# A decoder trunk's first 30 microseconds in another order: memory rows before the small tables, each half of them handled by itself

## The reference

```python
h = x + 0.5 * rms_norm(swiglu(rms_norm(x, n_ffn1_pre), ffn1_w_in, ffn1_w_out), n_ffn1_post)
m = token_mixing(rms_norm(h, n_mix_pre), ...)     # w_in, three branches, w_out
h = h + rms_norm(m, n_mix_post)
h = h + 0.5 * rms_norm(swiglu(rms_norm(h, n_ffn2_pre), ffn2_w_in, ffn2_w_out), n_ffn2_post)
```

## Time and profile before

| | |
|---|---|
| median of 3 runs | 1865.48 us (1864.84 to 1869.85) |
| the profiled execution, first to last instruction (its span) | 1861.5 us |
| PE busy | 1810.6 us, 97% |
| DVE busy | 1344.2 us, 72% |
| ACT busy | 902.9 us, 49% |
| DMA, mean over the span | 198 GB/s |

### The profile page before, as it was taken

One profiled execution on the slowest core, in us unless ns is written; L12 is line 12 of the kernel. 1 busy time (PEld: TensorE's weight loads), 2 busy tenths in 40 slices (PEclk: granted clock), 3 DMA queues, 4 the chain that ended last, 5 costly groups with the idle time before them and its releaser, 6 DMA issues.

```text
span 1861.5 us, 40412 instructions
## 1 busy us (share of the span) xinstructions
PE 1810.6 (97%) x16247; PEld 1746.6 (94%) x16247; DVE 1344.2 (72%) x2096; ACT 902.9 (49%) x1051; POOL 118.5 (6%) x174
## 2 busy tenths in 40 slices
PE   7999999999999999999999999999999899999998
PEld 6999999988989999999999999999889899989998
DVE  6777577787777868877577765868777776887764
ACT  5443354546574254543354434465567545354433
POOL 0000001111210100000000000010112010000000
PEclk9999999999999999999999999999999999999999
DMA  7776666766864656566667766676778465546654
GB/s 231 216 206 192 178 196 221 237 226 216 276 227 139 192 169 220 162 191 168 173 188 212 205 184 198 198 247 201 232 235 283 138 205 170 181 129 189 182 163 133
DMA packets 433619, 368.20 MB, mean 198 GB/s; under 512 B 9395, under 2 KB 411125, under 8 KB 432811
## 3 DMA queue, kind: packets, MB, share of 16 engines
q1 hardware_dynamic: 409560, 276.60, 50.0%
q0 software_dynamic: 23872, 89.03, 14.2%
HBM read 338.90 MB, written 26.69 MB: 196 GB/s over the span
## 4 chain that ended last, share of the span: by engine, by line
PE 71%; DVE 16%; issue 5%; ACT 4%; DMA 2%; DVEq 0%; SPq 0%; ACTq 0%
PE proj L686 46%; PE proj L709 4%; PE proj L704 4%; PE proj L705 4%; DVE wl L1859 3%; ACT wh L1364 2%; PE aux L749 1%; PE proj L660 1%; PE aux L919 1%; PE aux L1141 1%; PE aux L864 1%; PE aux L880 1%; DVE y L2053 1%; DVE x L2054 1%; DMA raw<-w_mem_v 1%
## 5 line engine op out<-in xcount | busy, mean ns | idle before, releaser
L1859 DVE TENSOR_TENSOR wl<-raw,wh 128x2048 fp32r<-128x2048 f32 (+1 forms) x280 | 599.2, 2140 | 193.2 <-ACT wh L1364 167.9
L1364 ACT CAST wh<-raw 128x2048 fp32r<-128x2048 f32 (+1 forms) x280 | 500.3, 1787 | 249.3 <-PE proj L686 105.9
L686 PE MATMUL proj<-xl,wh 128*128 128x264 f32 x2624 | 381.4, 286 | 1.9 <-DVEq L2009 1.3
L686 PE MATMUL proj<-xh,wh 128*128 128x264 f32 x2624 | 380.1, 287 | 0.0
L686 PE MATMUL proj<-xh,wl 128*128 128x264 f32 x2624 | 372.0, 284 | 1.8 <-DVE wl L1859 1.1
L686 PEld LDWEIGHTS proj<-xl,wh 128*128 128x128 f32 x2624 | 341.3, 188 | 15.5 <-issue 13.2
L686 PEld LDWEIGHTS proj<-xh,wl 128*128 128x128 f32 x2624 | 339.0, 188 | 4.2 <-DVE wl L1859 3.9
L686 PEld LDWEIGHTS proj<-xh,wh 128*128 128x128 f32 x2624 | 340.0, 188 | 3.1 <-issue 0.8
L705 PE MATMUL proj<-hl,wh 128*128 128x264 f32 x704 | 173.3, 283 | 0.0
L704 PE MATMUL proj<-hh,wh 128*128 128x264 f32 x704 | 173.0, 283 | 0.0
L1385 ACT ACTIVATE gate<-gate 128x264 f32<-128x264 f32 x88 | 37.4, 425 | 246.2 <-DVEq L1895 246.2
(11 more groups left out here) (477 smaller groups left out, 2271.5 us busy)
## 6 DMA issues: line engine op xcount, KB each, us to landing
raw<-ffn_w_in SPq DMA_DIRECT2D x176, 512.0 KB, 5.1
raw<-w_in SPq DMA_DIRECT2D x80, 1024.0 KB, 5.6
raw<-ffn_w_out SPq DMA_DIRECT2D x64, 704.0 KB, 4.6
sring<-cache_mem_k POOLq DMA_DIRECT2D x32, 512.0 KB, 5.1
sring<-cache_mem_v POOLq DMA_DIRECT2D x32, 512.0 KB, 4.0
out<-sring POOLq DMA_DIRECT2D x32, 512.0 KB, 4.5
sring<-state_gdn POOLq DMA_DIRECT2D x30, 512.0 KB, 5.1
raw<-w_mem_v SPq DMA_DIRECT2D x8, 1024.0 KB, 6.9
```

What stands on the lines that cost most here:

```text
L686: mm = pe.matmul(o, w[:, s, k * 256 + t * P:k * 256 + (t + 1) * P], a[:, k, :], **go)
L1364: act.copy(wh[:, slot, 0:size], raw[:, slot, 0:size]).then_inc(hi_done[slot], 1)
L1859: dve.tensor_sub(wl[:, slot, 0:size], raw[:, slot, 0:size], wh[:, slot, 0:size].bitcast(F32)).then_inc(split_done[slot], 1)
```

## The change

The memory rows are asked for first, in two transfers of 128 rows, the second with a semaphore of its own (`rows_loaded`). The ten small tables are asked for by ACT's queue instead of SP's, as ACT's first instructions. Each half of the rows is summed, rooted, inverted and scaled by itself: DVE does the whole of half zero and the sum of half one ahead of the copies of the gains, the rest of half one behind them. PE waits for each half by itself. Before the tables, PE runs eight products of `ones` with itself into a bank that nobody reads. `memhi` is told twice (after four tiles and after eight), and DVE's `meml` and PE's group zero wait for each half. Group zero now runs one part for both token tiles before the next part. Of the input, PE turns only four of the eight column blocks (two banks, `proj[2]` and `proj[3]`) ahead of group zero; the other four are turned into the same two banks behind it ("group one" in the change's own words), when DVE has copied the first. DVE's four copies of the input stand behind `meml`, two and two, with group one's remainder between them. Everything else only counts semaphores on, and one unused milestone is dropped.

```diff
         def _(sp):
-            for dst, src in [(ident[:], t_ident)] + [(grow[2 * k:2 * k + 2, :], n) for k, n in enumerate(norms)] + [
-                    (crow[:], gdn_conv_w.rearrange("l j c -> (l j) c")), (nrow[:], gdn_norm)]:
-                sp.dma_start(dst, src).then_inc(const_loaded, 16)
-
-            sp.dma_start(mnat[:], mem_prompt[0].rearrange("(t p) d -> p t d", p=P)).then_inc(ends_moved, 16)
+            for t in range(2):
+                sp.dma_start(mnat[:, t, :], mem_prompt[0, t * P:(t + 1) * P, :]).then_inc(rows_loaded if t else ends_moved, 16)
...
         def _(pe):
+            pe.wait_ge(pro_act, 1)
+            for _ in range(8):
+                pe.matmul(proj[1][:, 0:P], ones[:], ones[:], start=True, stop=True)
             pe.wait_ge(const_loaded, 16 * 10)
...
-            pe.wait_ge(pro_dve, 2)
-            for k in range(KT):
-                for t in range(2):
+            for t in range(2):
+                pe.wait_ge(pro_dve, 2 * t + 1)
+                for k in range(KT):
                     c = (k % 2) * NM + t * P
                     mm = pe.transpose(aux[:, k // 2, c:c + P], mnat[:, t, k * P:(k + 1) * P], ident[:])
             mm.then_inc(pro_pe, 1)
-            pe.wait_ge(const_loaded, 16 * 12)
-            for b in range(4):
-                for k in (2 * b, 2 * b + 1):
-                    for t in range(2):
-                        c = (k % 2) * SEQ + t * P
-                        mm = pe.transpose(proj[b][:, c:c + P], xnat[:, t, k * P:(k + 1) * P], ident[:])
-                mm.then_inc(pro_pe, 1)
-            pe.wait_ge(pro_dve, 4)
+
+            def input_rows(half):
+                for b in range(2):
+                    if half:
+                        pe.wait_ge(pro_dve, 4 + b)
+                    for k in range(2):
+                        for t in range(2):
+                            c = 4 * half + 2 * b + k
+                            mm = pe.transpose(proj[2 + b][:, k * SEQ + t * P:k * SEQ + (t + 1) * P], xnat[:, t, c * P:(c + 1) * P], ident[:])
+                    mm.then_inc(pro_pe, 1)
 
             def input_samples():
-                pe.wait_ge(pro_dve, 6)
+                pe.wait_ge(pro_dve, 7)
...
-                pe.wait_ge(pro_dve, 7)
+                pe.wait_ge(pro_dve, 8)
+            pe.wait_ge(const_loaded, 16 * 12)
+            input_rows(0)
...
             def memory_parts(part, k):
-                if part == HIGH and k == 0:
-                    pe.wait_ge(M["memhi"], 1)
+                if part == HIGH and k % 4 == 0:
+                    pe.wait_ge(M["memhi"], k // 4 + 1)
                 elif part == INPUT_LOW and k == 0:
                     pe.wait_ge(M["mem_split"], 1)
-            products(0, "mv0", memh, meml, "natural", early=memory_parts, groups=(0,))
+            products(0, "mv0", memh, meml, "natural", early=memory_parts, groups=(0,),
+                     parts_of={0: ((HIGH, 0, 8, None), (WEIGHT_LOW, 0, 8, None), (INPUT_LOW, 0, 8, None))})
+            input_rows(1)
             input_samples()
...
         def _(act):
+            for dst, src in [(ident[:], t_ident)] + [(grow[2 * k:2 * k + 2, :], n) for k, n in enumerate(norms)] + [
+                    (crow[:], gdn_conv_w.rearrange("l j c -> (l j) c")), (nrow[:], gdn_norm)]:
+                act.dma_start(dst, src).then_inc(const_loaded, 16)
...
-            act.wait_ge(pro_act, 2)
-            order(act.activation(srs[:], srs[:], ACT.Sqrt, bias=epst[:], scale=1.0 / D))
-            act.sem_inc(pro_act, 1)
+            for t in range(2):
+                act.wait_ge(pro_act, 2 * t + 2)
+                order(act.activation(srs[:, t:t + 1], srs[:, t:t + 1], ACT.Sqrt, bias=epst[:], scale=1.0 / D))
+                act.sem_inc(pro_act, 1)
...
-                order.wait()
-                act.sem_inc(M["memhi"], 1)
+                    if k % 4 == 3:
+                        order.wait()
+                        act.sem_inc(M["memhi"], 1)
...
         def _(dve):
+            def sum_rows(t):
+                dve.wait_ge(rows_loaded if t else ends_moved, 16)
+                order(dve.tensor_tensor_reduce(...))
+                dve.sem_inc(pro_act, 1)
+
+            def scale_rows(t):
+                dve.wait_ge(pro_act, 2 * t + 3)
+                order(dve.reciprocal(srs[:, t:t + 1], srs[:, t:t + 1]))
+                order(ts_(mnat[:, t, :], mnat[:, t, :], srs[:, t:t + 1], None, ALU.mult))
+                dve.sem_inc(pro_dve, 1)
+            sum_rows(0)
+            scale_rows(0)
+            sum_rows(1)
             dve.wait_ge(pro_pe, 1)
...
+            scale_rows(1)
...
-                dve.wait_ge(M["memhi"], layer + 1)
                 for k in range(KT):
+                    if k % 4 == 0:
+                        dve.wait_ge(M["memhi"], 2 * layer + k // 4 + 1)
...
-            input_rows((0, 1))
             split_memory(0, memh, meml)
+            input_rows(0)
             split(0, 1, 0, GW)
-            input_rows((2, 3))
+            input_rows(1)
```

More of the change, by code:

```diff
@@ L659, in group @@
                                         early(part, k)
[L660 to L661 removed]
+                                    go = dict(start=(c == 0 and k == first), stop=(c == len(pieces) - 1 and k == last - 1))
+                                    if kind == "natural":
+                                        mm = pe.matmul(proj[bank][:, 0:256], a[:, k, t * P:(t + 1) * P], w[:, s, k * 256:(k + 1) * 256], **go)
+                                    else:
+                                        mm = pe.matmul(proj[bank][:, 0:a.shape[2]], w[:, s, k * 256 + t * P:k * 256 + (t + 1) * P], a[:, k, :], **go)
                                 if c == len(pieces) - 1:
@@ L1459, in _ @@
             split(0, 0, 0, GW)
-            act.wait_ge(pro_dve, 1)
+            act.wait_ge(pro_dve, 2)
             act.wait_ge(pro_pe, 2)
@@ L1975, in _, with input_rows @@
             split(0, 0, 0, GW)
-            def input_rows(banks):
-                for b in banks:
-                    dve.wait_ge(pro_pe, 3 + b)
-                    order(cp(x[:, 2 * b:2 * b + 2, 0:SEQ], proj[b][:].rearrange("p (k t) -> p k t", k=2)))
+            def input_rows(half):
+                for b in range(2):
+                    dve.wait_ge(pro_pe, 3 + 2 * half + b)
+                    c = 4 * half + 2 * b
+                    order(cp(x[:, c:c + 2, 0:SEQ], proj[2 + b][:].rearrange("p (k t) -> p k t", k=2)))
                     dve.sem_inc(pro_dve, 1)
-            input_rows((0, 1))
             split_memory(0, memh, meml)
+            input_rows(0)
             split(0, 1, 0, GW)
-            input_rows((2, 3))
+            input_rows(1)
             dve.wait_ge(pro_pe, 7)
```

40 lines of the change are left out of this document (15 added, 25 removed).

## The result

The changed kernel is slower, by less than half a per cent.

| series | changed, median | before, median | ratio (95% interval) |
|---|---|---|---|
| first, 8 runs | 1871.22 us | 1865.62 us | 1.0029 (1.0020 to 1.0039) |
| second, 11 runs | 1866.88 | 1865.23 | 1.0014 (1.0005 to 1.0023) |
| third, 8 runs | 1869.10 | 1864.82 | 1.0023 (1.0013 to 1.0033) |

The account below looks back on a forecast made before the run. PE was taken as the bound, 97% busy, with time to be had only in the prologue's chain of waits. 4.95 less 0.4 plus 0.45 less 0.2 gave 4.8 us off 1865.48: 1860.7, range 1857.0 to 1865.3.

Parts of the forecast that it names:

- d: Landing of the ten small tables: delay past 6.25 us from sharing the DMA engines with the rows, taken as 0.4 us.
- the prediction's own chain: Prologue from gains to group one: `memh` at 13.05, `meml` done 18.0, group zero 21.5, group one 25.25 instead of 30.20.
- the clock's 0.45: Half one's turns on PE: early products bring 2.4 GHz forward, saving 0.9 us; half of it, 0.45, was counted.
- the 0.2 for hand-offs: Whole prologue: 0.2 us taken off the gain for added hand-offs.
- the handover: Group zero to group one: DVE becomes the limit, group one begins at 25.25, giving 2.55 us back.
- Hidden by the tables: Start of PE: the eight products of `ones` run 2.6 to 6.2 us, covered by the wait for the tables.
- what the prologue gains at this product is what the kernel gains: Group one's first product, 30.20 us before: order unchanged from there, so its gain is the kernel's if FFN weights come equally earlier.
- Tables late: Rival, prologue: tables share DMA with rows and weights or ACT issues slowly; d 5.8 gives 1866.5 us, decides from 4.75; chance 0.10.
- Clock early: Rival, prologue: PE at 2.4 GHz from the tables on, gain 6.0 us, time 1858.8 to 1859.5; chance 0.17.
- Lost at the FFN: Rival, FFN's first weights: landing does not move with the request, PE's rest grows 1.4 to 6.2 us, 1865.5; chance 0.08.
- It does not do what it says: Rival, memory rows: sums not done by 9.3 us, 1 us lost, 1861.7; no chance of its own given.
- the calmer DMA: FFN's first weights, added to the early-clock case: half of PE's 1.4 us rest also saved, 1858.8.

Follow-up runs that it names:

- halved tables: Changed kernel, five tables asked by SP ahead of the rows, five by ACT: 1864.78 us against 1865.23 (0.9999); without the eight products 1863.14 against 1864.82 (0.9994).
- the first eight lines of the table: Tables by ACT alone; three kernels without products; four padded by 64, 32 or 56 small products: time change within 1.2 us of the FFN's first product's shift.
- the changed kernel with one block more: Changed kernel with 56 small products behind its eight wide ones, 64 in all: 1865.80 us against before's 1865.58, ratio 1.0001 (0.9992 to 1.0010).
- Half a block: Kernel before with 32 small products of ones added ahead of the tables: 1865.43 us against 1865.58, ratio 1.0001 (0.9992 to 1.0010).

## Why the prediction was wrong, point by point

**The step that failed first: d, "the delay from sharing the DMA engines with the rows".** It was given 0.4 us, below both rows that it names (1.2 and 5.8), on the size of the tables and SP's pace of issuing. The issuing was priced right: ten requests took ACT from 0.75 to 4.34. The sharing was not. The last table landed 6.08 us after its request instead of 2.45, the tables were turned at 10.13, and d is 3.85. Put into the prediction's own chain, group one comes at 25.25 + 3.85 = 29.10; the profile has 29.11. With the two small terms of the sum it would be 28.85, so the tenth is in part luck: the clock's 0.45 did not come, and the 0.2 for hand-offs does not show. But the chain was right: rows summed under the tables, one half's work left behind the gains, `memh` and `meml` overlapping (18.56 + 3.34 ends 5.0 behind `memh`'s start, as 18.0 stands 4.95 behind 13.05), DVE's copies as the limit of the handover (group zero ends at 25.71, 0.4 later than 21.5 + 3.85, which this limit hides). The bound from `wab`, 8.3 us on POOL's queue, was the nearer one: small transfers beside a stream. I weighed it down because `rot_tab` had landed fast, but at the tables' requests the rows stream at that very moment: with the first weight held back they are still 2.6 us late, with five on each queue ahead of the rows not at all. The Trainium skill, DMA: Bandwidth & Descriptors, Issuing engines are not separate DMA queues, which the prediction cited for this rival, says that they interleave on the same DMA engines; the 6.08 us agree.

**The second: "The eight products of `ones`" were costed at nothing, "Hidden by the tables".** In place they are hidden (with halved tables they hold the turns up: 6.33 against 5.62 without them). They also shift PE's whole program by 32 instructions against its block reads, and that costs 1.7 to 2.5 us alone in the kernel before. The clock's 0.45 was meant as their gain, and it did not come: the memory's sixteen turns take 3.83 us (3.69 in the earlier trace rows), and but for the first of a half each takes 421 ns, as most in the earlier trace rows, the 1.2 GHz level, in half one as in half zero. The level rose in the input's turns behind them. What the products do give shows at group zero and group one, about 1.1 to 1.3 us with halved tables.

**The third follows from it: "what the prologue gains at this product is what the kernel gains".** The order of the instructions is unchanged from group one on, and this is true of the kernels in the first eight lines of the table. It fails where PE's program moves against the transfers. The profiled run of the changed kernel gains 1.1 us at the FFN's first product and is 8.7 longer in span than before's. From that product to the end, before and after:

```profile
48.70:1861.50 1812.80, 1777.21 (x15989) 1714.06 (x15989) 1315.60 (x2042) 877.50 (x1011) 114.71 (x165) 1.00 0.64 197
```
```profile
47.64:1870.20 1822.56, 1782.67 (x15989) 1717.84 (x15989) 1315.40 (x2042) 877.35 (x1011) 114.92 (x165) 1.00 0.64 196
```

Of the 9.8 us more, PE stands still for 4.3, and 3.3 of these are the waits of the two stages above. The other 5.5 are work: the same 15,989 products take longer, at a mean granted clock of 0.996 over the span against 0.998. One stretch of low clock stands right behind the longest wait, the 1.95 us before 1175.03:

```profile
1175.03:1178.00 2.97, 2.97 (x17) 2.13 (x18) 2.13 (x2) 2.18 (x2) 0.00 (x0) 0.50 0.15 30
```

There the products behind the wait run at the 1.2 GHz level, which adds to its cost. But such stretches stand in every profile, in before's as well, and the changed kernel with one block more had a mean of 0.9955 and no such loss (a part of its low clock lies in the prologue). How much of the lower clock the products cause, and why the three series differ, stay open.

**The bytes.** The prediction had weights in by 9 us and the input by 12, at 388 GB/s. In the changed kernel the cast waits for the weight until 11.47, and queues 1 and 10 move 221 GB/s over the first 10.2 us. It is no steady rate, as 40 slices of 0.255 us show:

```profile
GB/s 0 0 0 0 0 0 0 199 201 307 265 408 227 241 402 354 434 434 402 402 325 369 329 361 394 386 398 365 442 365 237 153 84 72 72 76 28 32 40 48
```

Nothing moves before 1.8 us, some 200 to 440 GB/s until 7.6, and from 8.2 on a tail of 28 to 84 in which the weight's last packets come; why this tail is so slow no run shows. With the tables out of the way the bytes are the next limit: 29.35 with all tables by SP, 27.03 halved, not 25.25.

**The rivals.** "Tables late" is what happened, with d at 3.85, not far from its 4.75; alone it would have left a gain of about 0.9 us, and the profile has 1.1 at group one. The slower side was reached by a mechanism that no rival named. "Clock early" did not happen: PE still takes 3.83 us for the memory's sixteen turns. "Lost at the FFN" fell: the rest is 1.43 us. "It does not do what it says" fell too: the sums are done by 9.2. The range that was drawn from the rivals does not follow from their sums: "Clock early" with the calmer DMA gives 1858.8, not 1857.0, and tables late by 4 give 4.95 - 4 - 0.2, so 1864.7, not 1865.3; all three measured medians lie above either. The 260 to 340 GB/s of "Lost at the FFN" are 261 to 304 in the earlier trace rows, which changes nothing.

**Marks of the prediction**: table turns at 6.3 to 7.0 (10.13, missed), `memh` at 12.5 to 13.8 (16.92, missed), group one between 24 and 26 (29.11, missed), the rest before the FFN 1.2 to 1.6 (1.43, kept). The first mark that it gave against itself, tables turned after 8 us, is the one that decided the prologue.

## What to carry to other kernels

Small tables on which everything waits are asked for ahead of any large transfer: on a second queue beside the stream they started as early here, and landed with the stream. Where a kernel streams weights with little slack, added or removed instructions on PE can move its block reads against the transfers; a difference of 0.1 to 0.3% that appears far from an edit should be tested by padding to a whole block before a cause is sought in the edit's place. Half a block did as well here, so what counts is which transfer is hit, and that has to be looked up. Compare the landing of one named transfer over several kernels: it showed here what medians of noisy runs could not.

## What was not expected of the hardware

PE's program is itself DMA traffic: 129 reads of 16 KB, 2.11 MB in this run, and 256 added instructions make 130. One such read early in a 1 MB weight transfer moved its landing from between 5.0 and 5.4 us to between 6.0 and 6.6; at the end of it the stream ran at a sixteenth of its rate, 26 of 390 GB/s.

Ten small requests on ACT's queue, begun while SP's queue moved 2 MB, landed 6.08 us after the last of them; with the first weight held back they were still 2.6 us late; with five of them on each queue and the rows behind, they were in by 5.40 to 5.59 us in three profiles, against 6.06 to 6.27 wherever SP asked for all ten ahead of the rows.
